# A two-layer hybrid decoder trunk on one core: layers written out, the next layer's input transposed inside the last down projection, weights stored in the order in which they are read, small parameters packed, gate columns moved into the first chunk

## The chip, the core and the metric

The kernel runs on one core of a Trainium2 chip. A core has five engines that run their own instruction streams and meet at semaphores: TensorE (PE, the matrix engine, with a separate row PEld for its weight loads), VectorE (DVE), ScalarE (ACT), GpSimd (POOL) and SyncE (SP). SP only starts DMAs here. The metric is the device time of one execution in microseconds (us); lower is better. The kernel before was timed three times: 2275.53, 2276.73 and 2278.32 us, median 2276.73 us.

## The reference

Input is x (256 tokens by 2048 features, float32), positions, and the parameters of two layers. One layer computes

```
n = rms_norm(x, attn_norm_w)
proj = n @ w_in                      # 2048 -> 6160 columns
   # gla q 512 | k 512 | v 1024 | g 1024 | gate_lr 16 | diff q 1024 | k 1024 | v 1024
y_gla  = gla_mixer(q, k, v, g, gate_lr @ gate_w2 + gate_b)    # chunks of 64 tokens
y_diff = diff_attention(...)         # rotary, softmax 1 - lambda * softmax 2
x = x + concat(y_gla, y_diff) @ w_out        # 2048 -> 2048
n = rms_norm(x, mlp_norm_w)
x = x + relu(n @ w_up)^2 @ w_down            # 2048 -> 8192 -> 2048
```

The 16 gate_lr columns are the low-rank input of the decay gates. All weights are float32 and are read once per execution.

## The kernel before

Each weight matrix is cut into chunks of 512 output columns, and a chunk into pieces of two blocks of 128 rows (KP = 2), 512 KB a piece. A layer has 384 pieces: 96 for w_in (12 chunks), 32 for w_out (8 half-height chunks), and 4 blocks of 64 for the MLP (4 up chunks and 4 down chunks of 8 pieces each).

Float32 accuracy comes from three single-pass products. For every piece SP loads `raw` (4 slots), ACT copies it to a rounded `w_high` (`split`, L656), DVE computes `w_low = raw - w_high` (L920), and PE does 2 row blocks x 2 token tiles x 3 matmuls of 128x512 (L356 to L358): high by high, high by low, low by high. A slot is free for ACT when PE has used the piece that was in it four pieces earlier, and free for SP when DVE has made its low half. The stationary operand is the transposed activation, also as high and low: `xt_high`, `xt_low` for w_in and w_up, `mt_high`, `mt_low` for w_out and w_down. To make it, PE transposes 512 columns of x (8 transposes, L391) into a `side` PSUM buffer, ACT writes the high half times the norm weight (`normed_high`, L682), DVE the low half (`normed_low`, L944). Sums stand in two PSUM accumulators that alternate by chunk; DVE takes them out (`take`, L967; `add_to_x`, L973; L1297).

The order of the work is written out by hand on each engine: `pieces(n)` means "do pieces up to n of this layer", and the attention work stands between such calls.

All engines run a loop over the two layers (`Fori(0, DEPTH)`); inside it the first MLP block is written out and the other three are a loop (`Fori(1, BLOCKS)`). Semaphore waits compare with values computed from the loop registers.

Start of a layer: SP first loads three rows of norm weights (L291), then the first four pieces, then eleven parameter DMAs (L303), among them the 16 gate columns `wlr` (128 KB in runs of 64 bytes) and gate_w2, norm weights and lambda vectors broadcast to 128 partitions; only then come pieces 4 and up. PE transposes the norm rows (L400), then x0 and x1, does pieces 0 and 1, transposes x2, pieces 2 and 3, transposes x3, pieces 4 to 7. DVE waits for all eleven parameter DMAs before it makes `w_low` of piece 2 (L980), ACT before piece 4 (L696). The squares of x for the norm (L706) come after piece 7, since they need the tile `tmp` that holds the lambda vectors.

The gate columns: 48 matmuls with 256 moving columns (L421 to L423) after piece 7, copied by ACT (L713), turned back with a small matmul (`lr_back`, L438), scaled on DVE, and transposed again (L445).

At the boundary of the layers everything above runs again: x1's last columns are ready only when DVE has added the last down chunk to x (L973), and the transposes of the next layer start after that. At the end of the program the last 512 columns of x are added by one DVE operation and stored by one DMA (L329).

Of the kernel before, what the change touches and what calls it, by code (L numbers as in the profile page):

```python
# [52 lines left out]
IN_AT = [c * CW for c in range(LR_COL // CW)] + [LR_COL + RANK + c * CW for c in range(6)]  # L53

CHUNKS = [(IN_CHUNK * c, IN_CHUNK, 0) for c in range(12)]
CHUNKS += [(12 * IN_CHUNK + HALF * k, HALF, (k // 4) * (KT // 2)) for k in range(8)]
MIX_PIECES = 12 * IN_CHUNK + 8 * HALF
BLOCKS = 4
BLOCK_PIECES = 8 * IN_CHUNK
LAYER_PIECES = MIX_PIECES + BLOCKS * BLOCK_PIECES  # L60
BLOCK_CHUNKS = 8
LAYER_CHUNKS = len(CHUNKS) + BLOCKS * BLOCK_CHUNKS

USES = ["nw", "x0", "x1", "x2", "x3", "lr", "gq", "lr_back", "lrT", "z", "gk", "diag"]
USES += [f"level{n}" for n in range(8)]
USES += ["go0", "go1", "dq0", "gy0", "gy1", "dq1", "dk0", "score0", "dk1", "score1", "w0", "score2",
         "do0", "w1", "score3", "do1", "w2", "do2", "w3", "do3", "dy0", "dy1", "m0", "m1", "m2", "m3"]
HUSES = 4 * BLOCKS  # L70
NUSES = len(USES) + HUSES
PAIR = {u: n % 2 for n, u in enumerate(USES)}
NTH = {u: n // 2 + 1 for n, u in enumerate(USES)}
PER_PAIR = [(NUSES + 1 - p) // 2 for p in range(2)]
LEVEL_AT = [27, 30, 33, 37, 41, 45, 49, 52]
NORM_DMAS = 3
PARAM_DMAS = 11
STEPS = {"dve": 160, "act": 40, "pool": 64}


def build(nc, ins, out):
    (x_d, pos_d, anw_d, win_d, w2_d, gb_d, onw_d, qnw_d, knw_d, lq1_d, lk1_d, lq2_d, lk2_d, sub_d,
     wout_d, mnw_d, wup_d, wdn_d, ident_d, maskb_d, lmask_d, scanm_d, invf_d, lamc_d) = ins
# [7 lines left out]
    raw = sb("raw", [P, SLOTS, KP, CW])  # L91
    w_high = sb("w_high", [P, SLOTS, KP, CW], F32R)
    w_low = sb("w_low", [P, SLOTS, KP, CW], F32R)
# [25 lines left out]
    lmask = sb("lmask", [P, 7 * 64 + P])  # L119
# [12 lines left out]
    nw_rows = sb("nw_rows", [36, P])  # L132
    nwt = sb("nwt", [P, 36])
    w2 = sb("w2", [RANK, GH * DK])
    wlr = sb("wlr", [P, KT, RANK])
    onw = sb("onw", [P, DV])
    subw = sb("subw", [P, 256])
    qknw = sb("qknw", [P, 2, P])
    lamc = sb("lamc", [P, 2])
    lam_s = sb("lam_s", [P, 2])  # L140
    lam_e = sb("lam_e", [P, 2])
    nlam = sb("nlam", [P, 1])
# [33 lines left out]
    const_in = sem("const_in")  # L176
# [3 lines left out]
    params_in = sem("params_in")  # L180
    out_in = sem("out_in")
    angle_ready = sem("angle_ready")
# [5 lines left out]
    wlr_h = sem("wlr_h")  # L188
    wlr_ready = sem("wlr_ready")
# [20 lines left out]
    merge_open = sem("merge_open")  # L210
    layer_open = sem("layer_open")
    load_open = sem("load_open")
# [4 lines left out]
    def full(u, layer):  # L217

        return side_full[PAIR[u]], layer * PER_PAIR[PAIR[u]] + NTH[u]

    def done(u, layer):

        return side_done[PAIR[u]], layer * PER_PAIR[PAIR[u]] + (NTH[u] + 1)

    def hpair(c):
        return (len(USES) + c) % 2

    def hnth(c, block, layer):

        p = hpair(c)  # L230
        first = (len(USES) + 1 - p) // 2 + c // 2 + 1
        return layer * PER_PAIR[p] + block * 2 + first

    class Chain:


        def __init__(self, eng, step, per_layer):
            self.eng, self.step, self.per_layer = eng, step, per_layer
            self.layer, self.before, self.n = 0, 0, 0

        def start_layer(self, layer, before):
            self.layer, self.before, self.n = layer, before, 0

        def __call__(self, ins):
            self.n += 1
            assert self.n <= self.per_layer
            ins.then_inc(self.step, 1)
            self.eng.wait_ge(self.step, self.layer * self.per_layer + (self.before + self.n))

        def end_layer(self):  # L250
            if self.per_layer > self.n:
                self.eng.sem_inc(self.step, self.per_layer - self.n)
# [10 lines left out]
    with nc.Block() as block:  # L263
# [3 lines left out]
        def _(sp):  # L267
            sp.dma_start(ident[:], ident_d).then_inc(ident_in, 16)
            win = win_d.rearrange("l (k p) n -> l p k n", p=P)
            wout = wout_d.rearrange("l (k p) n -> l p k n", p=P)  # L270
            wup = wup_d.rearrange("l (k p) n -> l p k n", p=P)
            wdn = wdn_d.rearrange("l (k p) n -> l p k n", p=P)

            def load(n, before, src):

                sp.wait_ge(low_ready, before + (n + 1))
                if n == 0:
                    sp.sem_inc(load_open, 1)
                sp.dma_start(raw[:, n % SLOTS], src).then_inc(raw_in[n % SLOTS], 16)

            with sp.Fori(0, DEPTH) as layer:

                sp.wait_ge(piece_used, layer * (LAYER_PIECES - 6 * SLOTS) + 1)

                def bc(ap):
                    return ap.partition_broadcast(P)
                for dst, src in (
                        (nw_rows[0:16, :], anw_d[layer].rearrange("(k p) -> k p", p=P)),
                        (nw_rows[16:32, :], mnw_d[layer].rearrange("(k p) -> k p", p=P)),
                        (nw_rows[32:36, :], gb_d[layer].rearrange("(k p) -> k p", p=P))):  # L290
                    sp.dma_start(dst, src).then_inc(norms_in, 16)  # L291
                before = layer * LAYER_PIECES
                for n in range(SLOTS):
                    load(n, before, win[layer, :, KP * n:KP * (n + 1), IN_AT[0]:IN_AT[0] + CW])
                for dst, src in (
                        (wlr[:], win[layer, :, :, LR_COL:LR_COL + RANK]),
                        (w2[:], w2_d[layer]),
                        (onw[:], bc(onw_d[layer])), (subw[:], bc(sub_d[layer])),
                        (qknw[:, 0, :], bc(qnw_d[layer])), (qknw[:, 1, :], bc(knw_d[layer])),
                        (lamc[:], bc(lamc_d[layer])),  # L300
                        (tmp[:, 0:128], bc(lq1_d[layer])), (tmp[:, 128:256], bc(lq2_d[layer])),
                        (tmp[:, 256:384], bc(lk1_d[layer])), (tmp[:, 384:512], bc(lk2_d[layer]))):
                    sp.dma_start(dst, src).then_inc(params_in, 16)  # L303
                for c, (first, count, k0) in enumerate(CHUNKS):
                    for i in range(count):
                        k = k0 + KP * i
                        if first + i < SLOTS:
                            continue
                        if c < 12:
                            src = win[layer, :, k:k + KP, IN_AT[c]:IN_AT[c] + CW]  # L310
# [24 lines left out]
        def _(pe):  # L335
            pe.sem_inc(piece_used, SLOTS)

            def piece(n, before, first, count, k0, left, parity, cidx):
# [3 lines left out]
                if i == 0:  # L342

                    pe.wait_ge(acc_done, cidx)
# [1132 lines left out]
```

## Time and profile before

| | |
|---|---|
| median of 3 runs | 2276.73 us |
| span of the profiled execution (first to last instruction) | 2275.6 us |
| lowest of the 3 runs | 2275.53 us |
| PE busy | 2245.0 us (99%), 10342 matmuls |
| DVE busy | 1325.5 us (58%) |
| ACT busy | 1018.9 us (45%) |
| POOL busy | 225.0 us (10%) |
| DMA | 410.67 MB, mean 180 GB/s |

How to read it: the matmuls are pipelined, so the duration of one (390 to 396 ns for 128x512) is longer than the distance between two starts, and the distance is what counts. "Idle before" is the time in which the engine did nothing ahead of the instruction, and the releaser is who ended it. [...] The span and the timed runs agree within 1.1 us.

### The profile page before, as it was taken

Reading aid. Unit: us, or ns where it says so; the run is one execution under the profiler, and the core shown is the slowest. Engines: PE = TensorE matmul, PEld = TensorE weight load, DVE = VectorE, ACT = ScalarE, POOL = GpSimd, SP = SyncE. Lnnn points to the kernel's source line nnn. Section 1 sums busy time; section 2 is a strip of 40 time slices with the busy share of each in tenths; the row PEclk is TensorE's granted clock in tenths of the full one; section 3 lists DMA queues with packets and bytes.
Section 4 is the critical chain, followed back from the end, with each engine's and each line's share of the span. In section 5 each row is a group of like instructions: output and inputs, shape, how many; then the busy total and the mean of one; then the engine's idle time right before and its main releaser. Section 6 shows DMA issues by size and latency. Waiting matters only on the chain.

```text
span 2275.6 us, 29971 instructions
## 1 busy us (share of the span) xinstructions
PE 2245.0 (99%) x10342; PEld 1869.6 (82%) x10342; DVE 1325.5 (58%) x1278; ACT 1018.9 (45%) x1246; POOL 225.0 (10%) x155
## 2 busy tenths in 40 slices
PE   6999999999999999999989999999999999999999
PEld 5888888888888888888878888888888888888887
DVE  4678775655455555555457787756555554555554
ACT  4544454544344344344345445545444443443442
POOL 0034720000000000000001356100000000000000
PEclk9999999999999999999999999999999999999999
DMA  6555655665665665665555656556656666656654
GB/s 206 155 171 153 176 167 171 181 185 190 192 188 189 194 185 186 192 187 189 191 142 166 175 148 178 166 176 185 184 188 193 185 192 192 188 185 193 185 188 161
DMA packets 219099, 410.67 MB, mean 180 GB/s; under 512 B 17672, under 2 KB 20176, under 8 KB 218992
## 3 DMA queue, kind: packets, MB, share of 16 engines
q1 hardware_dynamic: 217056, 406.54, 58.9%
q10 hardware_dynamic: 1936, 2.75, 0.4%
q8 instruction: 60, 0.98, 0.2%
q14 instruction: 47, 0.39, 0.1%
HBM read 407.15 MB, written 2.10 MB: 180 GB/s over the span
## 4 chain that ended last, share of the span: by engine, by line
PE 91%; POOL 4%; issue 3%; SPq 1%; DMA 0%; DVE 0%; ACT 0%; POOLq 0%; DVEq 0%; ACTq 0%
PE acc L356 29%; PE acc L358 29%; PE acc L357 29%; PE side L611 1%; PE side L391 1%; SPq L303 1%; PE side L481 1%; POOL tmp L1418 1%; POOL stage L1423 1%; POOL y L1376 1%; POOL tmp L1419 0%; POOL k_lev L1369 0%; DMA tmp<-in_diff_lambda_k 0%; POOL stage L1411 0%; POOL tmp L1421 0%
## 5 line engine op out<-in xcount | busy, mean ns | idle before, releaser
L920 DVE TENSOR_TENSOR w_low<-raw,w_high 128x1024 fp32r<-128x1024 f32 x768 | 993.9, 1297 | 853.6 <-ACT w_high L656 851.8
L656 ACT ACTIVATE w_high<-raw 128x1024 fp32r<-128x1024 f32 x768 | 812.7, 1060 | 1102.3 <-PE acc L358 1099.6
L356 PE MATMUL acc<-w_high,xt_high 128*128 128x512 f32 x1792 | 709.9, 396 | 16.1 <-DVE w_low L920 16.1
L358 PE MATMUL acc<-w_high,xt_low 128*128 128x512 f32 x1792 | 701.3, 391 | 0.0
L357 PE MATMUL acc<-w_low,xt_high 128*128 128x512 f32 x1792 | 700.6, 391 | 0.0
L356 PE MATMUL acc<-w_high,mt_high 128*128 128x512 f32 x1280 | 502.1, 392 | 0.0
L358 PE MATMUL acc<-w_high,mt_low 128*128 128x512 f32 x1280 | 498.9, 390 | 0.0
L357 PE MATMUL acc<-w_low,mt_high 128*128 128x512 f32 x1280 | 498.4, 389 | 0.0
L356 PEld LDWEIGHTS acc<-w_high,xt_high 128*128 128x128 f32 x1792 | 338.5, 189 | 85.6 <-DVE w_low L920 17.0
L358 PEld LDWEIGHTS acc<-w_high,xt_low 128*128 128x128 f32 x1792 | 338.0, 189 | 71.3
L357 PEld LDWEIGHTS acc<-w_low,xt_high 128*128 128x128 f32 x1792 | 338.7, 189 | 68.2
L358 PEld LDWEIGHTS acc<-w_high,mt_low 128*128 128x128 f32 x1280 | 240.3, 188 | 50.2
L357 PEld LDWEIGHTS acc<-w_low,mt_high 128*128 128x128 f32 x1280 | 240.5, 188 | 49.2
L356 PEld LDWEIGHTS acc<-w_high,mt_high 128*128 128x128 f32 x1280 | 240.4, 188 | 49.0
L1335 POOL TENSOR_TENSOR xrs<-xss,eps 128x2 f32<-128x2 f32 x4 | 0.8, 196 | 932.8 <-ACT tmp L706 772.4
L973 DVE TENSOR_TENSOR x<-acc,x 128x1024 f32<-128x1024 f32 x48 | 58.7, 1223 | 30.0 <-PE acc L358 30.0
L1297 DVE TENSOR_SCALAR stage<-acc,xrs 128x512 f32<-128x512 f32 x64 | 45.1, 747 | 12.9 <-PE acc L358 12.9
L944 DVE SCALAR_TENSOR_TENSOR xt_low<-side,nwt,xt_high 128x256 fp32r<-128x256 f32 x64 | 26.5, 477 | 31.0 <-ACT xt_high L682 26.8
L896 ACT ACTIVATE stage<-stage 128x1024 f32<-128x1024 f32 x32 | 34.0, 1062 | 12.3 <-DVE stage L1297 12.3
L1306 DVE TENSOR_TENSOR mt_low<-side,mt_high 128x1024 fp32r<-128x1024 f32 x32 | 39.0, 1218 | 0.0
L682 ACT ACTIVATE xt_high<-side,nwt 128x256 fp32r<-128x256 f32 x64 | 24.9, 474 | 26.8 <-PE side L391 26.8
L611 PEld LDWEIGHTS side<-ident,stage 128*128 128x128 f32 x256 | 29.8, 140 | 4.2
(160 smaller groups left out, 909.5 us busy)
## 6 DMA issues: line engine op xcount, KB each, us to landing
raw<-in_w_up SPq DMA_DIRECT2D x256, 512.0 KB, 3.7
raw<-in_w_down SPq DMA_DIRECT2D x256, 512.0 KB, 3.6
raw<-in_w_in SPq DMA_DIRECT2D x192, 512.0 KB, 3.8
raw<-in_w_out SPq DMA_DIRECT2D x64, 512.0 KB, 3.7
x<-in_x ACTq DMA_DIRECT2D x4, 512.0 KB, 7.4
out<-x SPq DMA_DIRECT2D x4, 512.0 KB, 5.1
lmask<-c_lmask ACTq DMA_DIRECT2D x1, 288.0 KB, 10.6
wlr<-in_w_in SPq DMA_DIRECT2D x2, 128.0 KB, 8.9
```

Of the source, the lines that this page charges most:

```text
L356: pe.matmul(o, a_high, w_high[:, s, kk, :], start=start, stop=False)
L357: pe.matmul(o, a_high, w_low[:, s, kk, :], start=False, stop=False)
L358: last = pe.matmul(o, a_low, w_high[:, s, kk, :], start=False, stop=stop)
L611: last = pe.transpose(side[p][:, j * SEQ + t * P:j * SEQ + (t + 1) * P], stage[:, c % 2, t, j * P:(j + 1) * P], ident[:])
L656: act.activation(w_high[:, n % SLOTS], raw[:, n % SLOTS], ACT.Copy).then_inc(high_ready, 1)
L682: last = act.activation(xt_high[:, 4 * c + j, :], s[:, j * SEQ:(j + 1) * SEQ], ACT.Copy, scale=nwt[:, w0 + 4 * c + j:w0 + 4 * c + j + 1])
L896: act.activation(stage[:, c % 2], stage[:, c % 2], ACT.Square).then_inc(relu_h, 1)
L920: dve.tensor_tensor(w_low[:, n % SLOTS], raw[:, n % SLOTS], w_high[:, n % SLOTS].bitcast(F32), ALU.subtract).then_inc(low_ready, 1)
L944: last = dve.scalar_tensor_tensor(out=xt_low[:, k, :], in0=s[:, j * SEQ:(j + 1) * SEQ], scalar=nwt[:, w0 + k:w0 + k + 1], in1=xt_high[:, k ...
L973: dve.tensor_tensor(cols, acc[parity][:], cols, ALU.add).then_inc(acc_done, 1)
L1297: last = dve.tensor_scalar(stage[:, c % 2, t, :], acc[c % 2][:, t, :], xrs[:, 1, t:t + 1], 0.0, ALU.mult, ALU.max)
L1306: dve.tensor_tensor(mt_low[:, 4 * c:4 * c + 4, :].rearrange("p a b -> p (a b)"), side[hpair(c)][:], mt_high[:, 4 * c:4 * c + 4, :].rearran ...
```

## The change

It does five things.

1. The loops over layers and MLP blocks are gone: every engine's stream is written out, and every semaphore wait compares with a constant.
2. In the last MLP block of layer 0, PE transposes columns 0 to 1535 of the next layer's x (x0, x1, x2) in the middle of the last three down chunks, with ACT's and DVE's halves of it behind. Only x3 is left for after the last down chunk, and PE does piece 0 of the next layer before it. The squares of x come after piece 3, not after piece 7.
3. The host stores each weight matrix so that a piece is one contiguous run per partition (4 KB). The memory distance between two partitions of one piece becomes the whole length of a layer's row: 385 KB for w_in, 128 KB for w_out, 512 KB for w_up and w_down. Before, a piece was 256 runs of 2 KB, with rows 24, 8, 32 and 8 KB apart.
4. Norm weights come transposed and packed (one DMA, no PE transpose); the four broadcast parameters come as one `wide` tile, the lambda vectors as one 512 KB tile already repeated for 128 partitions. All but the norms are issued by POOL, most of them after PE has used three pieces. The DMAs of layer 1's parameters are issued during layer 1 after its first norm.
5. The 16 gate columns stand in front of w_in's columns. The first 528 columns (16 gate, 512 q) become two chunks of 264 columns, each in 4 pieces of 4 row blocks. Piece numbers from 8 on mean the same columns as before. `lr` and `lr_back` are gone; DVE takes the gate columns from the accumulator, and PE transposes them once (lrT).

At the end the last add and the last store are split by token tile. The core of the diff:

```diff
-IN_AT = [c * CW for c in range(LR_COL // CW)] + [LR_COL + RANK + c * CW for c in range(6)]
+Q_HALF = (CW - RANK) // 2
+SLOT = 4 * (RANK + Q_HALF)
+IN_AT = [0, RANK + Q_HALF] + [RANK + CW * (c + 1) for c in range(11)]
+IN_N = [RANK + Q_HALF, CW - Q_HALF] + [CW] * 11
+    chunks = [("in", IN_AT[c], IN_N[c], 0, KT, 4 if c < 2 else KP) for c in range(13)]
...
@@ sync
-            with sp.Fori(0, DEPTH) as layer:
-                sp.wait_ge(piece_used, layer * (LAYER_PIECES - 6 * SLOTS) + 1)
...
+            sp.dma_start(norms[:].rearrange("p l k -> p (l k)"), norms_d).then_inc(norms_in, 16)
+            def load(n):
+                layer, (c, k, kp) = n // LAYER_PIECES, PIECES[n % LAYER_PIECES]
+                name, at, cols, k0, _, _ = CHUNKS[c]
+                rows = KT * BLOCKS if name == "down" else KT
+                first = at * rows + (k0 + k) * cols
+                if n >= SLOTS:
+                    sp.wait_ge(low_ready, n - SLOTS + 1)
+                sp.dma_start(raw[:, n % SLOTS, 0:kp * cols],
+                             weights[name][layer, :, first:first + kp * cols]).then_inc(raw_in[n % SLOTS], 16)
+            load(0)
+            sp.dma_start(ident[:], ident_d).then_inc(ident_in, 16)
+            for n in range(1, DEPTH * LAYER_PIECES):
+                load(n)
@@ tensor
-                s = open_side("lr")
-                pe.wait_ge(wlr_ready, layer + 1)
-                for k in range(KT):
-                    pe.matmul(s[:, 0:SEQ], mt_high[:, k, 0:P], xt_high[:, k, :], start=k == 0, stop=False)
...
+                if layer == 0:
+                    pe.wait_ge(ident_in, 16)
+                    for c in range(3):
+                        pe.wait_ge(x_in[c], 16)
+                        transpose_chunk(f"x{c}", x[:, :, c * CW:(c + 1) * CW])
+                        if c:
+                            pieces(c, {c - 1: f"x{c - 1}"})
+                    pe.wait_ge(x_in[3], 16)
+                else:
+                    pieces(1, {0: "x0"})
+                    pe.wait_ge(*taken(layer - 1, LAYER_CHUNKS - 1))
                 transpose_chunk("x3", x[:, :, 3 * CW:4 * CW])
+                pieces(4, {n: f"x{n}" for n in range(4)})
+                pieces(8)
                 chunk_taken(0)
                 s = open_side("lrT")
...
+                            if i == 3 and c >= 5 and blk == BLOCKS - 1 and layer + 1 < DEPTH:
+                                chunk_taken(LAYER_CHUNKS - 9 + c)
+                                transpose_chunk(f"x{c - 5}", x[:, :, (c - 5) * CW:(c - 4) * CW], layer + 1)
@@ scalar
+                if layer == 0:
+                    act.wait_ge(norms_in, 16)
+                    for c in range(4):
+                        normed_high(f"x{c}", c, 0, 0)
+                        pieces(c + 1)
+                else:
+                    pieces(3)
+                    normed_high("x3", 3, 0, layer)
+                    pieces(4)
+                    act.wait_ge(*taken(layer - 1, LAYER_CHUNKS - 1))
                 for t in range(T):
                     act.activation(squared(t), x[:, t, :], ACT.Square, ...).then_inc(x_ss, 1)
+                    pieces(5 + t)
@@ vector
+                else:
+                    pieces(3)
+                    add_to_x(layer - 1, LAYER_CHUNKS - 1, 3)
+                    pieces(4)
+                    normed_low("x3", 3, 0, layer)
+                pieces(7)
                 dve.wait_ge(x_rs, layer * 2 + 1)
+                dve.wait_ge(*summed(layer, 0))
+                for t in range(T):
+                    dve.tensor_scalar(lr_s[:, t, :], acc[parity(layer, 0)][:, t, 0:RANK], ...)
+                    last = dve.tensor_scalar(stage[:, 0, t, 0:Q_HALF], ...)
+            for t in range(T):
+                xs = x[:, t, 3 * CW:]
+                dve.tensor_tensor(xs, acc[...][:, t, :], xs, ALU.add).then_inc(last_half, 1)
@@ gpsimd
+            pool.dma_start(lamc[:].rearrange("p l m -> p (l m)"), lamc_d).then_inc(lamc_in, 16)
+            pool.dma_start(att[:, 0:1024], lam_d).then_inc(lam_in, 16)
+            pool.wait_ge(piece_used, SLOTS + 3)
+            pool.dma_start(w2[:], w2_d[0]).then_inc(w2_in, 16)
...
+            pool.dma_start(maskb[:], maskb_d).then_inc(maskb_in, 16)
```

## Rows read from the trace of the kernel before

**Rows 1.** Busy time by stretch: stretch, length, then busy (count) per engine, clock, DMA, GB/s.
```profile
13.00:56.60 43.60, 33.79 (x161) 28.59 (x162) 23.17 (x35) 20.62 (x30) 1.79 (x3) 0.92 0.62 184
56.60:1143.40 1086.80, 1086.30 (x4996) 904.00 (x4994) 638.33 (x603) 487.17 (x588) 108.80 (x70) 1.00 0.60 181
1143.40:1184.20 40.80, 34.61 (x179) 29.54 (x179) 24.45 (x36) 22.01 (x35) 1.79 (x3) 0.87 0.55 155
```
**Rows 2.** Waits of the whole span: who waited for whom, total us, times, longest.
```profile
ACT w_high L656 <- PE acc L358: 1099.6, 698, 3.5
PE acc L356 <- DVE w_low L920: 16.1, 3, 7.1
PE side L400 <- DMA nw_rows<-in_gla_gate_b: 8.9, 1, 8.9
ACT w_high L656 <- DMA raw<-in_w_in: 2.4, 4, 1.1
```
**Rows 3.** Timeline, PE alone, 43 to 57 us: start, length, engine, line.
```profile
43.33 0.39 PE L356 MATMUL acc<-w_high,xt_high 128*128 128x512 f32 x1
...
50.13 0.39 PE L356 MATMUL acc<-w_high,xt_high 128*128 128x512 f32 x1
...
50.81 0.28 PE L421 MATMUL side<-xt_high,mt_high 128*128 128x256 f32 x1
50.81 0.19 PEld L422 LDWEIGHTS side<-xt_low,mt_high 128*128 128x128 f32 x1
...
56.20 0.28 PE L421 MATMUL side<-xt_high,mt_high 128*128 128x256 f32 x1
```
**Rows 4.** Timeline of the first 35 us.
```profile
6.82 11.19 SPq L303 DMA_DIRECT2D w<-in_gla_gate_w  x1
9.21 3.65 PE L391 MATMUL side<-ident,x 128*128 128x128 f32 x16
12.85 1.66 DVE L944 SCALAR_TENSOR_TENSOR xt_low<-side,nwt,xt_high 128x256 fp32r<-128x256 f32 x4 [12.85 <-ACT xt_high L682]
14.42 2.35 DVE L920 TENSOR_TENSOR w_low<-raw,w_high 128x1024 fp32r<-128x1024 f32 x2
14.43 1.06 ACT L656 ACTIVATE w_high<-raw 128x1024 fp32r<-128x1024 f32 x1 [0.67 <-DMA raw<-in_w_in]
15.39 1.55 ACT L682 ACTIVATE xt_high<-side,nwt 128x256 fp32r<-128x256 f32 x4
15.69 0.80 PE L356 MATMUL acc<-w_high,xt_high 128*128 128x512 f32 x1 [2.84 <-DVE w_low L920]
...
17.14 0.63 PE L356 MATMUL acc<-w_high,xt_high 128*128 128x512 f32 x1
...
18.42 0.63 PE L356 MATMUL acc<-w_high,xt_high 128*128 128x512 f32 x1
...
23.90 1.03 PE L391 MATMUL side<-ident,x 128*128 128x128 f32 x8
...
29.99 0.43 DVE L980 TENSOR_TENSOR tmp<-tmp 128x256 f32<-128x256 f32 x1 [11.36 <-DMA tmp<-in_diff_lambda_k]
...
32.05 0.79 PE L356 MATMUL acc<-w_high,xt_high 128*128 128x512 f32 x1 [7.12 <-DVE w_low L920]
```
**Rows 5.** DMA issues: x in the first 1.3 us, w_up over the span.
```profile
x<-in_x ACTq DMA_DIRECT2D x2, 512.0 KB, 5.9
...
raw<-in_w_up SPq DMA_DIRECT2D x256, 512.0 KB, 3.7
```
**Rows 6.** Timeline around the layer boundary.
```profile
1148.99 1.66 DVE L944 SCALAR_TENSOR_TENSOR xt_low<-side,nwt,xt_high 128x256 fp32r<-128x256 f32 x4 [4.23 <-issue]
...
1151.84 0.80 PE L356 MATMUL acc<-w_high,xt_high 128*128 128x512 f32 x1 [6.16 <-DVE w_low L920]
```
**Rows 7.** Timeline: the gate's way back (PE), and the program's end (DVE).
```profile
63.00 0.61 PE L438 MATMUL side<-ident,lr_t 16*128 16x16 f32 x4
...
2271.14 1.22 DVE L973 TENSOR_TENSOR x<-acc,x 128x1024 f32<-128x1024 f32 x1 [8.56 <-PE acc L358]
```

More of the change, by code:

```diff
@@ L425, in _ @@
-                last.then_inc(full_sem("lr"), 1)
-                pieces(10)
-                def chunk_taken(c):
-                    pe.wait_ge(acc_done, layer * LAYER_CHUNKS + (2 + c + 1))
-                chunk_taken(0)
-                transpose_chunk("gq", stage[:, 0])
-                s = open_side("lr_back")
-                pe.wait_ge(*done("lr", layer))
-                for t in range(T):
-                    last = pe.matmul(s[:, t * CW:t * CW + RANK], lr_t[:, t * P:(t + 1) * P],
-                                     ident[0:RANK, 0:RANK], start=True, stop=True)
@@ L440, in _, with chunk_taken @@
[L440 to L441 removed]
+                    last.then_inc(full_sem(u, of), 1)
+                def chunk_taken(c):
+                    pe.wait_ge(*taken(layer, c))
+                if layer == 0:
+                    pe.wait_ge(ident_in, 16)
+                    for c in range(3):
+                        pe.wait_ge(x_in[c], 16)
[6 more added lines that the diff above has]
+                    pe.wait_ge(*taken(layer - 1, LAYER_CHUNKS - 1))
@@ L925, in _ @@
+            for layer in range(DEPTH):
                 at = [0]
@@ new lines, in _ @@
+                last.then_inc(acc_done, 1)
+                pieces(9)
+                if layer == 0:
+                    dve.wait_ge(lamc_in, 16)
+                    dve.wait_ge(lam_exp, 1)
+                    for of in range(DEPTH):
+                        dve.scalar_tensor_tensor(out=nlam[:, of:of + 1], in0=lam_e[:, of, 1:2],
+                                                 scalar=lamc[:, of, 0:1], in1=lam_e[:, of, 0:1],
+                                                 op0=ALU.subtract, op1=ALU.subtract)
@@ L1016, in _ @@
-                c3 = float(np.float32(two_pi - c1 - c2))
-                for c in (c1, c2, c3):
-                    link(dve.scalar_tensor_tensor(out=ang, in0=turns, scalar=-c, in1=ang,
-                                                  op0=ALU.mult, op1=ALU.add))
-                pieces(14)
-                s = source("lr_back")
-                for t in range(T):
-                    last = dve.tensor_scalar(lr_s[:, t, :], s[:, t * CW:t * CW + RANK],
-                                             xrs[:, 0, t:t + 1], None, ALU.mult)
```

814 lines of the change are left out of this document (375 added, 439 removed).

## The prediction, made before the changed kernel was run

> **What bounds the kernel now.** I read the busy time by stretch first, cut at the places that the change touches. From 56.6 to 1143.4 us PE is busy 1086.30 of 1086.80 us at clock 1.00; the second layer's same stretch has the same length. The two stretches in which a layer starts are different: 13.0 to 56.6 us has 33.79 of 43.60 us busy at clock 0.92, 1143.4 to 1184.2 us has 34.61 of 40.80 at 0.87 [rows 1]. So the rest of the program is the count of matmuls times their distance, and only these two places, the end, and the number and width of the matmuls can move the time. The waits say the same: ACT waits 1099.6 us for PE to free a slot and 2.4 us for weight DMAs, and PE's own waits on `w_low` are 16.1 us in 3 times, all at layer starts [rows 2]. DVE and ACT cost nothing where they have cover.
>
> The price of a matmul is its distance to the next. Thirty 128x512 matmuls lie between the starts 43.33 and 50.13: 226.7 ns each. Forty-five of 256 columns lie between 50.81 and 56.20: 119.8 ns each [rows 3]. The difference, 106.9 ns for 256 columns, is 0.4176 ns a column, so 264 columns come to 119.8 + 8 x 0.4176 = 123.1 ns. A PE transpose chunk of eight inside a stream costs about 0.80 us: seven distances of 0.109 us and the two changes of kind, from the eight that take 1.03 us with the last one's drain [rows 4].
>
> **Start, part by part.** Before, the work of the first accumulator chunk and the gate ends at 56.56, just after the last row of [rows 3]. In it are 96 x 0.2267 + 48 x 0.1198 = 27.5 us of matmuls and 1.6 us of transposes; the rest is waiting and the half clock (the starts 17.14 and 18.42 are three matmuls apart, 427 ns each) [rows 4]. What held it: PE waited for the norm rows until 8.9 us [rows 2], 2.84 us for the first `w_low`, and 7.12 us at 32.05, since DVE stood until 29.99 for the lambda DMAs; those came late because SP stood 11.19 us on issue 6.82, behind the 64-byte gate columns [rows 4]. Written so, the next waits are these. x0 landed some 5.9 us after an issue at 0.7 to 1.3 [rows 5], so x0's transposes can start near 6.5 instead of 9.21, with `ident` and the norms as one DMA in by then. From there I step with the durations of [rows 4]: eight cold transposes 1.8 (half of 3.65), ACT's high half 1.6, DVE's low half 1.7, DVE's `w_low` 1.2 to 1.3 (half of 2.35, for 1056 elements 3% more): piece 0 at about 13.0 instead of 15.69. Piece 0 is 24 x 0.22 = 5.3 us at the half clock. x2's transposes stand behind it, then piece 1 (24 x 0.1231 = 2.95 us), x3's, and pieces 2 and 3 each wait for the chain ACT 1.6, DVE 1.7, DVE 1.3 behind the transposes: they start near 24.4 and 28.2, with 1 us lost ahead of each. Pieces 4 to 7 need 11.8 us more, the two squares on ACT and the products of lambda on DVE lie in the 2.95 us of a piece. Chunk 1 ends at 28.2 + 2.95 + 11.8 = 43.0. That is 13.6 us less; 3.9 us of it is plain PE work: 192 x 0.1231 = 23.6 against 27.5.
>
> What could be late next here: POOL issues seven DMAs between piece 2 and its rsqrt for `xrs`, and DVE waits for `xrs` before it takes chunk 0, with `w_low` of piece 7 queued behind, and PE behind that. In the trace POOL issues none. The nearest issues are those of SP and ACT, 0.3 to 0.9 us, with one of 11.19 [rows 4]. Seven at the short end end before x's squares do and cost 0. If each took 2 us, `xrs` would be some 5 us late for piece 7. I take 0, nearest to the ordinary issue, and keep 0 to 5. Landing order adds: the lambda tile is 512 KB instead of 256, beside x and the first pieces, but `lmask`, `maskb` and `scanm` leave this window; I keep -1 to +4 for it.
>
> **Layer boundary.** Before: 40.8 us from the last down matmul to the end of the gate [rows 1], with 6.16 us of waiting: DVE makes the low half at 1148.99 after 4.23 us in which nothing that the profile shows held it, and PE restarts at 1151.84 on the half clock [rows 6]. After: PE goes from the last down matmul into piece 0, whose x0 was made three chunks earlier; DVE adds x's last columns (1.22 us, [rows 7]) in piece 0's 2.95 us. x3's transposes end at 3.75, piece 1 at 6.7, piece 2 at 9.65; x3's halves are ready after ACT 1.6, ACT `w_high` 1.1, DVE `w_low` 1.3 and DVE 1.7, in that order on the two engines: about 9.6. That is a tie; I take 0.3 us of stall and keep 0 to 1.5. So the stretch is 192 x 0.1231 + 0.80 + 0.3 = 24.7 us, 16.1 us less; the other three transpose chunks move into the last down chunks, where each has whole pieces of cover on ACT and DVE, and cost PE 3 x 0.80 = 2.4. Net -13.7 us. No idle time means no half clock. In layer 1 DVE waits for `wide` after piece 8; POOL issues it after the rsqrt at about 13 us past the boundary, DVE comes there at 18, and PE would feel it at 24.5: covered, and with 3 us over it even if the landing is doubled.
>
> [...]
>
> **Smaller parts.** `lr_back`: four tiny matmuls and two changes of kind, 0.70 us a layer (start 63.00, the next weight matmul 0.55 us later, and a dearer step before it) [rows 7]: -1.4 us. The written-out MLP blocks, constant waits and the packed norms after the start: 0, covered by a busy PE; a gain is excluded by the 0.5 us that PE is idle in 1086.8 [rows 1], a loss only if instructions come late. Last add and store by halves: the 1.22 us add [rows 7] releases its first half after 0.65, the second store is half as large; -0.5, between 0 and -1. Contiguous weight runs: 0, because landing takes 3.7 us [rows 5] and ACT waits for PE and not for data [rows 2]; below nothing is excluded by the same waits, above see the rival.
>
> **Sum,** against the profiled execution (span 2275.6 us, which the timed runs exceed by -0.1 to 2.7, the median by 1.1): -13.6 -13.7 -1.4 -0.5 = -29.2, so a span of 2246.4. With the median's 1.1 us, and 0.5 us for the half of the POOL and landing bounds that I don't dismiss, I predict **2248 us**.
>
> **Rivals.**
> (a) *The start gives back part.* POOL's issues or the landing of x and pieces 0 to 3 decide: +4 to +10, so 2252 to 2258; for it: everything in the first 15 us shares one set of DMA engines, and POOL's issue price is unknown. Against: less data is wanted early than before.
> (b) *The boundary doesn't do what it says.* If the fetch of code, not the loop end, held DVE for 4.23 us, or x3's chain is longer, PE waits once more and drops to the half clock: up to 6 us of stall and 3 us of slow matmuls come back, 2257.
> (c) *Narrow matmuls are held by weight loads.* A load is shown with 0.19 us [rows 3]. At 190 ns instead of 123 the 384 narrow ones cost 384 x 0.067 = 26 us more, and the time is 2274. Against: the 256-column ones run at 119.8 ns beside the same 0.19 us loads, so loads overlap.
> (d) *Slower: the new memory distances.* [...] A piece lasts PE 12 x 0.2267 = 2.72 us, so 193 GB/s are needed; the kernel runs at 181 with 0.60 of the DMA engines' time [rows 1], so there is room up to about 300. It decides only if the rate falls by more than a third. At 183 GB/s, 5% short, each of the 512 MLP pieces takes 0.14 us longer: +73, a time of 2321. Against: nothing in the trace; for it: it can't be seen there, since the old rows were 8 to 32 KB apart.
>
> [...]
>
> **Chances.** The forecast 0.75 (own range 2242 to 2254), (a) 0.10, (b) 0.04, (c) 0.03, (d) 0.06, and 0.02 for another loss such as late instructions. The range 2241 to 2259 leaves (c), (d) and the edges out, and takes in POOL's 5, landing's -1 to 4 and the boundary's 1.5. No change means within 0.2%, 4.6 us, about what a measurement of this kernel can tell. Faster by more: the first three cases, 0.89. Within: (c), 0.03, and a little of the rest, 0.04. Slower: (d) and late instructions, 0.07.
>
> **What would show it.** The stretch to the first 512-column matmul after the gate columns ends near 43 us instead of 56.6, with POOL's last DMA issue ahead of its first rsqrt; narrow matmuls start 0.123 us apart; x3's chunk stands 3 us after the last down matmul and PE's clock stays at 1.00 there; PE waits for `w_low` under 3 us in all; weight pieces land in about 3.7 us for w_up and w_down too, and ACT still waits for PE. A landing of over 8 us in the MLP, or ACT waiting for DMAs there, would prove (d) and the forecast wrong; a long middle stretch (over 1089 us) with PE idle would too.

## The result and the profile after

The changed kernel takes 2281.31 us (median of 18 runs, 2280.33 to 2282.22) against 2277.85 us for the kernel before (18 runs, 2275.53 to 2279.65). The ratio is 1.0016, 95% interval 1.001 to 1.0023: slower by 0.16%, within the 0.2% that the prediction called no change. I had forecast 2248 us. The profiled execution has a span of 2279.2 us.

Here is the busy time by stretch of the changed kernel, cut at the same places in the work as [rows 1]: start to the end of the narrow chunks, the rest of layer 0, the second layer's narrow chunks, the rest of layer 1. The columns are those of [rows 1].

```profile
13.00:46.90 33.90, 28.09 (x211) 27.69 (x211) 22.51 (x36) 20.62 (x32) 6.55 (x10) 0.90 0.61 211
46.90:1150.00 1103.10, 1103.10 (x5015) 905.89 (x5013) 646.91 (x619) 494.07 (x602) 108.42 (x70) 1.00 0.54 180
1150.00:1174.50 24.50, 24.50 (x203) 24.43 (x202) 13.82 (x18) 13.41 (x16) 2.99 (x5) 1.00 0.56 191
1174.50:2275.00 1100.50, 1100.50 (x4991) 903.19 (x4988) 633.49 (x588) 484.78 (x584) 108.92 (x70) 1.00 0.54 178
```

The two places that were to be mended are mended: the start ends at 46.9 instead of 56.6 us, the layer boundary takes 24.5 us instead of 40.8, with PE busy throughout at clock 1.00 (before, the clock stood at 0.50 from 1149 to 1156 us). The loss is in the two long stretches, where only +1.7 and -0.7 us were to happen: 1103.1 and 1100.5 us instead of 1086.8 each [rows 1]. PE isn't idle there at all, and weight loads are busy for 903 to 906 us as before (904). So it isn't a wait that was added: the same matmuls take longer. The waits of the changed kernel (who waited for whom, total us, times, longest) leave no other place. PE itself waits little; what has grown is ACT's wait for PE, from 1099.6 us [rows 2]:

```profile
ACT w_high L593 <- PE acc L334: 1136.9, 702, 3.5
PE side L362 <- DMA ident<-c_ident: 9.3, 1, 9.3
PE acc L332 <- DVE w_low L849: 6.3, 3, 4.7
ACT w_high L593 <- DMA raw<-in_w_in: 3.0, 2, 1.7
```

The distance between two starts shows it. This is PE's timeline of the changed kernel from 603 us: one piece in slot 3, then the start of the next, in slot 0 (start, length, engine, line).

```profile
603.28 0.40 PE L332 MATMUL acc<-w_high,mt_high 128*128 128x512 f32 x1
603.52 0.39 PE L333 MATMUL acc<-w_low,mt_high 128*128 128x512 f32 x1
...
604.67 0.40 PE L332 MATMUL acc<-w_high,mt_high 128*128 128x512 f32 x1
604.91 0.39 PE L333 MATMUL acc<-w_low,mt_high 128*128 128x512 f32 x1
605.14 0.40 PE L334 MATMUL acc<-w_high,mt_low 128*128 128x512 f32 x1
605.38 0.39 PE L332 MATMUL acc<-w_high,mt_high 128*128 128x512 f32 x1
...
606.07 0.39 PE L332 MATMUL acc<-w_high,xt_high 128*128 128x512 f32 x1
606.31 0.40 PE L333 MATMUL acc<-w_low,xt_high 128*128 128x512 f32 x1
...
607.00 0.39 PE L333 MATMUL acc<-w_low,xt_high 128*128 128x512 f32 x1
607.22 0.39 PE L334 MATMUL acc<-w_high,xt_low 128*128 128x512 f32 x1
607.45 0.39 PE L332 MATMUL acc<-w_high,xt_high 128*128 128x512 f32 x1
607.68 0.39 PE L333 MATMUL acc<-w_low,xt_high 128*128 128x512 f32 x1
```

The piece in slot 3 takes 606.07 - 603.28 = 2.79 us for 12 matmuls, with distances that alternate between 0.24 and 0.22 or 0.23; from its fourth matmul on the next piece goes on at 0.227. Averaged from the start times of this trace over 600 to 1000 us, the distance is 227.9, 232.7, 228.1 and 232.6 ns in slots 0 to 3, and 226.7 to 227.2 in all four before. These means leave out the nine steps of some 313 ns in that stretch at which PE comes back from other work. The change made a slot 1056 elements long (4 row blocks of 264 columns), 4224 bytes, where it was 4096. So slots 1 and 3 start 128 bytes off a multiple of 256, counted from the start of the tile. I saw no other property that tells odd from even slots; whether it is the cause is for the experiments.

### The profile page after: what moved, and what is told of

The parts are those of the page before. It is cut to its first block, busy times and chain, and to the rows that moved or that the text cites. A ratio compares the mean times of both kernels' runs of the same rounds, so it can differ in the third digit from the quotient of the medians.

```text
span 2279.2 us, 25481 instructions
## 1 busy us (share of the span) xinstructions
PE 2259.6 (99%) x10428; PEld 1864.2 (82%) x10428; DVE 1318.0 (58%) x1263; ACT 1014.5 (45%) x1235; POOL 228.5 (10%) x164
## 4 chain that ended last, share of the span: by engine, by line
PE 99%; DMA 0%; DVE 0%; ACT 0%; issue 0%; SPq 0%; DVEq 0%; ACTq 0%
PE acc L332 31%; PE acc L334 31%; PE acc L333 31%; PE side L362 1%; PE side L552 1%; PE side L427 1%; DMA ident<-c_ident 0%; PE side L479 0%; PE side L398 0%; PE side L412 0%; PE side L478 0%; PE side L496 0%; PE side L447 0%; PE side L498 0%; PE side L445 0%; PE side L439 0%
## 5 line engine op out<-in xcount | busy, mean ns | idle before, releaser
L849 DVE TENSOR_TENSOR w_low<-raw,w_high 128x1024 fp32r<-128x1024 f32 (+1 forms) x768 | 993.1, 1295 | 889.1 <-ACT w_high L593 888.2
L593 ACT ACTIVATE w_high<-raw 128x1024 fp32r<-128x1024 f32 (+1 forms) x768 | 813.3, 1061 | 1139.9 <-PE acc L334 1136.9
L332 PE MATMUL acc<-w_high,xt_high 128*128 128x512 f32 (+1 forms) x1856 | 723.4, 390 | 6.3 <-DVE w_low L849 6.3
L334 PE MATMUL acc<-w_high,xt_low 128*128 128x512 f32 (+1 forms) x1856 | 716.3, 386 | 0.0
L333 PE MATMUL acc<-w_low,xt_high 128*128 128x512 f32 (+1 forms) x1856 | 714.9, 385 | 0.0
L332 PEld LDWEIGHTS acc<-w_high,xt_high 128*128 128x128 f32 x1856 | 349.9, 188 | 77.7 <-issue 7.5
L334 PEld LDWEIGHTS acc<-w_high,xt_low 128*128 128x128 f32 x1856 | 349.3, 188 | 73.8
L333 PEld LDWEIGHTS acc<-w_low,xt_high 128*128 128x128 f32 x1856 | 349.9, 189 | 71.6
L899 DVE TENSOR_TENSOR x<-acc,x 128x1024 f32<-128x1024 f32 x47 | 57.5, 1223 | 13.6 <-PE acc L334 13.6
L862 DVE SCALAR_TENSOR_TENSOR xt_low<-side,norms,xt_high 128x256 fp32r<-128x256 f32 x64 | 26.5, 478 | 24.0 <-ACT xt_high L605 24.0
L552 PE MATMUL side<-ident,stage 128*128 128x128 f32 x256 | 33.1, 272 | 0.0
```

Source lines behind the costliest of these rows:

```text
L332: pe.matmul(o, a_high, w_high[:, n % SLOTS, w], start=start, stop=False)
L333: pe.matmul(o, a_high, w_low[:, n % SLOTS, w], start=False, stop=False)
L334: last = pe.matmul(o, a_low, w_high[:, n % SLOTS, w], start=False, stop=stop)
L552: last = pe.transpose(s[:, j * SEQ + t * P:j * SEQ + (t + 1) * P], stage[:, c % 2, t, j * P:(j + 1) * P], ident[:])
L593: act.activation(w_high[:, n % SLOTS, 0:size], raw[:, n % SLOTS, 0:size], ACT.Copy).then_inc(high_ready, 1)
L849: dve.tensor_tensor(w_low[:, n % SLOTS, 0:size], raw[:, n % SLOTS, 0:size], w_high[:, n % SLOTS, 0:size].bitcast(F32), ALU.subtract).then_ ...
```

## The experiments

Each was compared with the kernel before on the same chip. Addresses stand in no view: where I give a tile's start, it is an estimate from the tile sizes, with each tile directly behind the one before it in the kernel's text and `raw` on a multiple of 256. Where I give the mean distance, it is that between main matmuls, averaged as above from the trace's start times over 600 to 1000 us. Over all slots it is 226.8 ns in the kernel before and 230.3 in the changed kernel; their difference is the 3.5 ns from which the expectations up to e4 are worked out. The same can be read without arithmetic from the count of matmuls that PE starts in this stretch, in brackets behind its busy time. These are the kernel before, the changed kernel and e1_w1088:

```profile
600.00:1000.00 400.00, 400.00 (x1802) 332.06 (x1801) 208.78 (x180) 170.73 (x163) 0.00 (x0) 1.00 0.62 189
600.00:1000.00 400.00, 400.00 (x1776) 326.97 (x1775) 206.11 (x179) 168.46 (x160) 0.00 (x0) 1.00 0.56 187
600.00:1000.00 400.00, 400.00 (x1803) 331.89 (x1802) 209.04 (x181) 170.64 (x163) 0.00 (x0) 1.00 0.57 189
```

**e1_w1088, only the slot pitch mended.**

```diff
-    w_high = sb("w_high", [P, SLOTS, SLOT], F32R)
-    w_low = sb("w_low", [P, SLOTS, SLOT], F32R)
+    w_high = sb("w_high", [P, SLOTS, 1088], F32R)
+    w_low = sb("w_low", [P, SLOTS, 1088], F32R)
```

> The changed kernel with one number changed: the slots of w_high and w_low lie 1088 elements (4352 bytes) apart instead of 1056 (4224), so that every slot starts on a multiple of 256 bytes; raw keeps 1056. In the changed kernel's trace the 512-column matmuls are 232.6 ns apart in slots 1 and 3 (start 128 bytes off a multiple of 256) and 227.9 in slots 0 and 2. Theory A, the start address of the moving operand costs it: all slots near 226.8 ns, 9024 matmuls x 3.5 ns = 32 us less, about 2250 us. Theory B, the new memory layout of the weights (runs of 4 KB) or the fetch of the written-out code slows TensorE: no change, 2281. Theory C, the pitch of raw, which DMA writes and ACT and DVE read, disturbs TensorE: no change, 2281.

Measured: 2251.98 us, ratio to before 0.9892 (0.9875 to 0.9908). Mean distance 226.8 ns (226.7 to 227.2 by slot); the odd slots, 256 bytes off a multiple of 512, aren't slower. The long stretches are back, and the rest is as in the changed kernel (busy time by stretch of this run):

```profile
13.00:46.80 33.80, 27.93 (x209) 27.53 (x210) 22.51 (x36) 20.69 (x32) 6.55 (x10) 0.90 0.61 203
46.80:1135.30 1088.50, 1088.14 (x5015) 905.81 (x5013) 648.32 (x619) 494.02 (x602) 108.92 (x70) 1.00 0.57 182
1135.30:1159.60 24.30, 24.30 (x203) 24.23 (x202) 13.81 (x18) 13.40 (x16) 2.99 (x5) 1.00 0.59 195
1159.60:2245.40 1085.80, 1085.42 (x4991) 903.13 (x4988) 634.99 (x588) 484.70 (x584) 108.92 (x70) 1.00 0.56 181
```

Raw kept its pitch, and the memory layout and the written-out code stayed: rivals B and C fall for the changed kernel.

This run also shows where no cost appears. In the narrow chunks a row block is 1056 bytes long, so blocks 1 to 3 of a piece start 32, 64 and 96 bytes off. In this run's narrow chunks at the layer boundary, matmuls of blocks 0 to 3 stand 122.0, 121.0, 120.6 and 121.7 ns from the next (averaged from the start times): the offset blocks aren't slower. In the changed kernel, with 128 bytes more in the odd slots, the mean of these matmuls is 122.2 ns against 121.3 here. So what follows is measured for 512 columns.

**e2_before_w1056, the same fault put into the kernel before.** The tiles become one flat row with a pitch.

```diff
-    w_high = sb("w_high", [P, SLOTS, KP, CW], F32R)
-    w_low = sb("w_low", [P, SLOTS, KP, CW], F32R)
+    w_high = sb("w_high", [P, 3 * 1056 + 1024], F32R)
+    w_low = sb("w_low", [P, 3 * 1056 + 1024], F32R)
...
```

> The kernel before with its w_high and w_low slots 1056 elements apart instead of 1024, and nothing else. Theory A: slots 1 and 3 go to 232 to 234 ns, slots 0 and 2 stay at 226.8 to 228, 9216 x 3.5 ns = 32 us more, about 2309 us. Theory B (memory layout, code): no change, 2277. Theory C (raw): no change.

Measured: 2309.35 us, ratio 1.0145 (1.0128 to 1.0162). The size is right, the picture isn't: slots 0 to 3 are at 230.6, 228.7, 232.6 and 230.8 ns, so the even slots, which theory A wants fast, are slow too. The mean over all slots is 230.7 ns, and 1769 matmuls start from 600 to 1000 us, against 1802 before. The tile sizes tell what else moved, by the estimate above: w_high's tile is now 16768 bytes, 128 off a multiple of 256, so w_low behind it starts 128 bytes off, and its even slots are the offset ones; behind both tiles x, xt and mt are back on multiples of 256. In every slot one of the two w tiles is off. That the time hit theory A's number is therefore no proof of A: half of the pairs are off in either picture.

**e3_before_raw1056, only raw's pitch.**

```diff
-    raw = sb("raw", [P, SLOTS, KP, CW])
+    raw = sb("raw", [P, 3 * 1056 + 1024])
...
```

> The kernel before with only raw's slots 1056 elements apart. Theory A: no change, 2277 within 2 us. Theory C: about 30 us more, with slots 1 and 3 slow.

Measured: 2276.82 us, ratio 0.9998 (0.9988 to 1.0008), distance 226.8 ns, with slots 1 and 3 at 226.7. C falls here as well. But this run says more than I had planned. Raw's tile is 16768 bytes, 128 off a multiple of 256, so by the same estimate w_high, w_low, xt and mt all start 128 bytes off. All moving operands are off, and nothing is slow. Theory A as I put it is refuted.

**e4_before_low1056, only w_low's pitch.**

```diff
-    w_low = sb("w_low", [P, SLOTS, KP, CW], F32R)
+    w_low = sb("w_low", [P, 3 * 1056 + 1024], F32R)
...
```

> The kernel before with only w_low's slots 1056 elements apart, so one matmul in three has a moving operand 128 bytes off in slots 1 and 3. Theory A: a third of the 32 us, about +10 us (2287), and in the trace the distance after the w_low matmuls of odd slots is longer. If instead one badly placed operand disturbs its neighbours as much, up to +30.

Measured: 2314.0 us, ratio 1.0163 (1.0146 to 1.018); slots 0 to 3 at 231.8, 231.0, 231.8 and 230.6 ns, 231.3 over all, with 1765 matmuls from 600 to 1000 us. A third of the moving operands got the new pitch, and the loss is larger than with all of them, outside both numbers that I had given. The estimate from the sizes offers a reason: w_low's tile pushes xt and mt 128 bytes off, and now all pairs with w_high and those with w_low's even slots disagree, five in six.

**e5_stat128, the stationary operands moved instead.** From here on the theory (A2) is that the distance modulo 256 between the two operands counts.

```diff
+    pad = sb("pad", [P, 32])
...
```

It stands between w_low and x, and nothing reads it.

> The kernel before with an unused tile of 128 bytes per partition between w_low and x, so that x, xt and mt move by 128 bytes and the weight slots stay on multiples of 256 bytes. The run with only raw's pitch changed had moved w_high, w_low, xt and mt together by 128 bytes off a multiple of 256 and was not slower, so theory A as I put it (the moving operand's own start) doesn't hold alone. Theory A2, it is the distance modulo 256 bytes between the moving operand (w) and the stationary one (xt, mt): all slots slow, between 231 ns (even slots of the run with w_low's pitch changed) and 233.4 ns (odd slots of the changed kernel), +4.5 to +6.6 ns x 9216 = +41 to +61 us, about 2318 to 2338. Theory A, the moving operand's own start counts: no change, 2277.

Measured: 2324.25 us, ratio 1.0208 (1.0191 to 1.0225), all four slots at 232.2 to 232.6 ns. An unused tile of 128 bytes costs 47 us. A2 holds, A doesn't. The same stretch from 600 to 1000 us, this run first, e3_before_raw1056 second; busy PE and clock say nothing, the count and the weight loads' busy time do:

```profile
600.00:1000.00 400.00, 400.00 (x1757) 325.23 (x1756) 202.75 (x175) 165.29 (x158) 0.00 (x0) 1.00 0.60 185
```

```profile
600.00:1000.00 400.00, 400.00 (x1802) 331.97 (x1802) 208.77 (x180) 170.64 (x162) 0.00 (x0) 1.00 0.61 189
```

**e6_w1040 and e7_w1032, how far off is off.** Both w tiles get a pitch of 4160 or 4128 bytes and a length of 4160 elements (16640 bytes), so that what follows stays on multiples of 256.

```diff
+    w_high = sb("w_high", [P, 4160], F32R)
+    w_low = sb("w_low", [P, 4160], F32R)
+    RAW, HIGH, LOW = 1024, 1040, 1040
...
```

In e7_w1032 the last two numbers are 1032.

> The kernel before with w_high and w_low slots 1040 elements (4160 bytes) apart, each tile padded so that w_low and xt start on multiples of 256 bytes: slots 0 to 3 are 0, 64, 128 and 192 bytes off xt modulo 256. A2 with a grain of 64 bytes or less: slot 0 at 226.7 ns, slot 2 as the odd slots of the changed kernel (232 to 233), slots 1 and 3 slow as well by some amount. A2 with a grain of 128 bytes only: slots 1 and 3 like a neighbour. Time 2290 to 2320 us.

> As the run before, with 1032 elements (4128 bytes): slots 0 to 3 are 0, 32, 64 and 96 bytes off. If any offset that isn't 0 modulo 256 costs, slots 1, 2 and 3 are all near 232 ns and the time is 2277 + 9216 x 0.75 x 5 ns = 2312. If only 128 costs, all are at 226.8 and the time is 2277.

Measured, one run each: 2313.85 and 2319.01 us. Distances by the slot's offset to xt:

```
offset modulo 256 bytes   0      32     64     96     128    192
ns between starts, e6     228.7         230.3         232.7  233.0
ns between starts, e7     229.8  233.6  229.9  234.2
```

Slot 0 is slow only in its earlier matmuls, as in the timeline above, behind a slow slot; its last ones are at 226.7. So a slot's mean holds something of the slot before it, and the figures are no exact price of one offset. Every offset tried costs 3 to 7.5 ns a matmul, and 32 and 96 cost most. e7 missed its 2312 us by 7, upwards: slots 1 and 3 cost more than the 5 ns that I had put, and slot 0 wasn't free. e6 is inside its range.

**e8_no_early_turn, the moved transposes undone in the aligned kernel.**

```diff
-                            if i == 3 and c >= 5 and blk == BLOCKS - 1 and layer + 1 < DEPTH:
...
-                                chunk_taken(LAYER_CHUNKS - 9 + c)
-                                transpose_chunk(f"x{c - 5}", x[:, :, (c - 5) * CW:(c - 4) * CW], layer + 1)
...
-                    pieces(1, {0: "x0"})
                     pe.wait_ge(*taken(layer - 1, LAYER_CHUNKS - 1))
+                for c in range(3):
+                    pe.wait_ge(x_in[c], 16)
+                    transpose_chunk(f"x{c}", x[:, :, c * CW:(c + 1) * CW])
...
```

ACT and DVE change with it.

> The aligned kernel (slots 1088 apart) with the second layer started as the first: x0 to x3 are transposed after the last down chunk, and the squares stay after piece 3. It undoes only the moved transposes. Theory: they are worth 10 to 14 us (restart some 7 us after the last down matmul, half clock for a few us, 1 us of wait ahead of pieces 2 and 3, against 2.4 us more of transposes in the down chunks), so 2262 to 2266 against 2252. Rival: they are worth nothing, since the chain through DVE and ACT is as long either way: 2252.

Measured: 2261.43 us, ratio 0.9929 (0.9912 to 0.9946): the moved transposes are worth 9.5 us beside e1 (two chips; the spans differ by 9.7), a little under the range. By stretches of the two traces it is 12.6 us less at the boundary and 2.7 us more in the down chunks. PE's timeline at the boundary (with what ended the idle time) shows the wait that comes back, and the granted clock falls: it is 0.50 from 1140.0 to 1144.8 us, where the matmuls of 264 columns stand 0.22 apart:

```profile
1134.03 1.97 PE L362 MATMUL side<-ident,x 128*128 128x128 f32 x16 [1.39 <-DVE x L886]
1139.87 0.56 PE L332 MATMUL acc<-w_high,xt_high 128*128 128x264 f32 x1 [3.87 <-DVE w_low L836]
```

The boundary stretch is 37.1 us here, against 41.1 in the kernel before, so 4.0 of its 16.5 us come from the rest of the change. The gate columns in the first chunks account for it alone: 192 narrow matmuls instead of 96 of 512 columns and 48 of 256 were to save 3.9 us of PE work. Written-out code and fewer, earlier parameters show no gain of their own at the boundary.

**e9_aligned_again.** The kernel of e1 once more, beside the next two.

> The aligned kernel again (the changed kernel with w_high and w_low slots 1088 elements apart), beside the next two on the same chip: 2252 us within 1.

Measured: 2251.09 us, ratio 0.9887 (0.9871 to 0.9904).

**e10_start, the start in order.**

```diff
+            sp.dma_start(ident[:], ident_d).then_inc(ident_in, 16)
             sp.dma_start(norms[:].rearrange("p l k -> p (l k)"), norms_d).then_inc(norms_in, 16)
...
             load(0)
-            sp.dma_start(ident[:], ident_d).then_inc(ident_in, 16)
...
+            act.wait_ge(const_ready, 1)
+            act.activation(junk[:, 0, 0:8], eps[:], ACT.Copy)
...
+            pool.wait_ge(piece_used, SLOTS + 1)
             pool.dma_start(att[:, 0:1024], lam_d).then_inc(lam_in, 16)
```

> The aligned kernel with three things moved at the start: ident is the first DMA (in the changed kernel it landed at 9.2 us behind the first weight piece, while x0 was in at 5.4), the 512 KB of lambda vectors are issued after PE has used piece 0, and one small activation ahead of the first wait loads ACT's table (1.28 us that stood between x0's transposes and their high half). Theory, the start is a chain and not a rate: x0's transposes at 5.6 instead of 9.3, piece 0 at 12 to 13 instead of 17.3, 3 to 5 us less than the aligned kernel: 2247 to 2249. Rival, the start is bound by the landing of x and the first pieces at 400 GB/s: no more than 1 us, 2251.

Measured: 2246.01 us (2245.34 to 2246.72), ratio 0.9864 (0.9848 to 0.9881): 5.1 us less than e9 on the same chip, and the fastest version, 31 us ahead of the kernel before. The forecast of 3 to 5 us is met at its upper end, and the rival's 1 us isn't. The rate that the rival names is in the traces (406, 398, 381 and 413 GB/s in the steps of 2 us from 6 to 14 us of the changed kernel; 384, 411 and 420 from 8 to 14 here), and the start got shorter all the same. The three edits were made together, so their shares aren't separated. The changed kernel's first matmuls and this run's:

```profile
9.27 3.28 PE L362 MATMUL side<-ident,x 128*128 128x128 f32 x16 [9.27 <-DMA ident<-c_ident]
17.29 0.56 PE L332 MATMUL acc<-w_high,xt_high 128*128 128x264 f32 x1 [4.75 <-DVE w_low L849]
```

```profile
2.79 1.28 ACT L584 ACT_TABLE_LOAD   x1 [2.79 <-issue]
4.97 1.94 PE L362 MATMUL side<-ident,x 128*128 128x128 f32 x8 [4.97 <-DMA x<-in_x]
11.80 0.56 PE L332 MATMUL acc<-w_high,xt_high 128*128 128x264 f32 x1 [2.44 <-DVE w_low L851]
```

**e11_old_layout, the memory layout undone in the aligned kernel.**

```diff
-                rows = KT * BLOCKS if name == "down" else KT
-                first = at * rows + (k0 + k) * cols
...
-                sp.dma_start(raw[:, n % SLOTS, 0:kp * cols],
-                             weights[name][layer, :, first:first + kp * cols]).then_inc(raw_in[n % SLOTS], 16)
+                src = weights[name].rearrange("l (k p) n -> l p k n", p=P)
+                sp.dma_start(raw[:, n % SLOTS, 0:kp * cols].rearrange("p (k n) -> p k n", k=kp),
+                             src[layer, :, k0 + k:k0 + k + kp, at:at + cols]).then_inc(raw_in[n % SLOTS], 16)
...
```

> The aligned kernel with the weight matrices in memory as before (only the gate columns moved to the front of w_in), so that a piece is again 256 runs of 2 KB, or 512 of 1 KB for the narrow chunks. It undoes the layout part alone. Theory, the transfers have cover either way: landing goes from 3.4 back to 3.7 us and the time stays at 2252 within 2. Rival, the new layout is worth something through the start or through TensorE's reads beside DMA writes: over 3 us slower, 2255 or more.

Measured: 2253.07 us, ratio 0.9897 (0.9881 to 0.9914), 2.0 us over e9, as forecast. The ratios' intervals overlap, but both hold the spread of the kernel before; the four runs of each version on this chip don't (2252.42 to 2253.67 against 2250.83 to 2251.14), so the new layout seems to be worth 1 to 2 us. In the single traces it lies at the start: piece 0 starts 1.6 us later (18.98 against 17.38), the first 512-column matmul 1.3 us later, and the stretches behind are equal. The w_up pieces land as in [rows 5]:

```profile
raw<-in_w_up SPq DMA_DIRECT2D x256, 512.0 KB, 3.7
```

**e12_low_stationary, who disturbs whom.**

```diff
+    pad0 = sb("pad0", [P, 32])
     xt_low = sb("xt_low", [P, KT, SEQ], F32R)
+    pad1 = sb("pad1", [P, 32])
```

> The kernel before with 128 unused bytes ahead of xt_low and 128 behind it: xt_low alone is 128 bytes off, xt_high, mt and all weight slots are on multiples of 256 bytes. In the w_in and up chunks every third matmul (L360 here, high weights by xt_low) has an offset stationary operand; the w_out and down chunks have none and are the control at 226.7 ns. If the weight load of a matmul is disturbed by, and disturbs, the matmul that streams meanwhile, the distance from the w_low matmul before it (L359) to it grows, by 5 to 20 ns; if it is the matmul with the offset operand itself, the distance from L360 to the next L358 grows. Time 2277 + 5376/3 x 5 to 20 ns: 2286 to 2313 us.

Measured, one run: 2296.97 us. The timeline of PE in an up chunk, where every third stationary operand (xt_low, L360) is off:

```profile
700.26 0.40 PE L359 MATMUL acc<-w_low,xt_high 128*128 128x512 f32 x1
700.49 0.40 PE L360 MATMUL acc<-w_high,xt_low 128*128 128x512 f32 x1
700.72 0.39 PE L358 MATMUL acc<-w_high,xt_high 128*128 128x512 f32 x1
700.95 0.40 PE L359 MATMUL acc<-w_low,xt_high 128*128 128x512 f32 x1
701.18 0.40 PE L360 MATMUL acc<-w_high,xt_low 128*128 128x512 f32 x1
```

From 600 to 1000 us the means are: L359 to L360 232.4 ns, L360 to L358 234.0, L358 to L359 227.1; with mt in the down chunks of the same run 226.6, 226.9 and 226.5. So both distances beside the offset operand grow, and the test doesn't choose between the weight load that runs beside the stream of the matmul before and the one that runs beside its own. It does show, in one run, that only the matmuls next to the offset operand pay.

## Why the prediction was wrong

Set against e1_w1088, which differs from the changed kernel by nothing but the pitch, the steps of the prediction come out so (starts of the main matmuls in the traces):

| step | predicted | measured |
|---|---|---|
| start, to the first piece after the narrow chunks | 56.6 to 43.0, -13.6 | to 46.8, -9.7 |
| rest of layer 0: lr_back out, three transpose chunks in | +1.7 | 1086.55 to 1088.26, +1.7 |
| layer boundary | 24.7 us, -16.1 | 41.07 to 24.53 (24.70 in the changed kernel), -16.5 |
| rest of layer 1: lr_back | -0.7 | 1086.53 to 1085.52, -1.0 |
| the end | -0.5 | 4.89 to 4.42, -0.5 |
| distance of the 512-column matmuls | unchanged, 0 | changed kernel against e1: +14.6 and +14.7 |

**The step that failed** is the premise in the first paragraph of the prediction, that outside the mended places "the rest of the program is the count of matmuls times their distance", with the distance taken from [rows 3] and kept. The count was right and the distance wasn't: between 600 and 1000 us 226.8 became 230.3 ns, and over the two long stretches the loss is 29.3 us, 3.2 ns in each of 9024 matmuls, while e1's other steps add up to -26.0. Together +3.3, and the spans differ by 3.6; the rest is 0.2 at the boundary and 0.1 at the start. None of the rivals had it either, and the sign named for a wrong forecast, a middle stretch of over 1089 us, came with PE busy and not idle. I had listed what each edit adds, moves and takes away in time, but not what it does to addresses: `SLOT = 4 * (RANK + Q_HALF)` stood in the diff, and I read it as room for wider pieces.

**The start** was the second miss: its gain was over-estimated by 3.9 us. With the pitch mended the kernel takes 2252 us where 2248 was forecast. The term that was off is "`ident` and the norms as one DMA in by then": x0 landed in time, at 5.4, but ident was issued behind the first weight piece and landed at 9.2, and ACT's table load of 1.28 us, which the sum has nowhere, now stood behind that wait. PE waited for `w_low` 6.3 us in all, 4.7 of it ahead of piece 0; I had named under 3 as the sign of being right. e10 puts both right and starts piece 0 at 11.8, where I had 13.0. The half clock that the prediction puts at the start before is read from distances alone, 427 ns a matmul [rows 4] against 226.7 [rows 3]: the clock column gives 1.00 from 15 to 20 us of that trace. In the changed kernel it gives 0.50 from 16 to 22 us, with matmuls of 264 columns 0.22 us apart.

**What held.** The narrow matmuls' 123.1 ns: they stand 122.2 apart at the changed kernel's boundary and 121.3 at e1's, so rival (c) didn't come. The +1.7 for the rest of layer 0 was met by luck: `lr_back` was worth 1.0 and not 0.7, as layer 1 shows, so the three transpose chunks cost about 2.7 and not 2.4, and the two errors cancel. POOL's seven DMAs took 0.52 to 0.57 us each, and its rsqrt at 35.5 us was in time, so rival (a)'s POOL part didn't come; its other half, late landing, is the start's miss, though what landed late was ident and not x0 or piece 0. Rival (b) didn't come. What held DVE for 4.23 us before [rows 6] no run shows; in e8, with x0's transposes behind the last add again, DVE stands 2.92 us there, and ACT's high half ends it. Rival (d) didn't either: with 512 KB between partitions the up and down pieces land in 3.4 us instead of 3.7, the changed kernel has ACT waiting 3.0 us for data in all, and e11 without the new layout isn't faster. So at a mean of 180 GB/s no run shows a cost of partitions 512 KB apart. Code written out cost nothing that shows: e1 carries all of it, with the long stretches as short as the sum has them.

**The mechanism, and what stays open.** Shown, with the addresses estimated from the tile sizes: the cost follows the difference of the start addresses of moving and stationary operand modulo 256 bytes (e3 moves both, 226.8 ns and no cost; e5 moves one, 232.4 ns and 47 us; 256 bytes in e1, 226.8 ns and no cost), and it is paid by the matmuls beside the offset operand (e12: 232.4 and 234.0 ns, against 227.1 for the third distance). Not shown: what in the chip makes the two operands' addresses matter to each other, whether offsets under 32 bytes matter, why the distances alternate as they do, and what sets the size. The pair alone doesn't set it: in e2 slots 0 and 2 have the same offsets and stand at 230.6 and 232.6 ns. ACT's and DVE's work on the weight slots is no rival: e5 and e12 leave raw and both w tiles where they were.

## What to carry to other kernels

When a tile's size changes, write down the start address modulo 256 bytes of every operand that TensorE reads, for every buffer of a rotation and for every tile behind it; here the change saved 26.0 us of waits and work and lost 29.3 us with its slots 128 bytes off. In a kernel with PE busy at 99%, compare the distance between two matmul starts, or the count in a fixed stretch, since PE's busy time and clock look the same with 1757 matmuls in 400 us as with 1802. At a kernel's start follow one chain (identity, first input tile, table load, first piece) and order the DMAs by it.

## What the runs showed of the hardware that I had not expected

Matmuls of 128x512 in float32r (the kernel's rounded high and low halves) with a new stationary operand each stand 226.8 ns apart on average if moving and stationary operand agree modulo 256 bytes by the tile sizes (the kernel before, e1, e3), and 230 to 234 ns apart if they don't (offsets of 32, 64, 96, 128 and 192 bytes; e5, e6, e7). PE's busy time, its waits and the granted clock hide it; the weight loads' busy time in a fixed stretch (325 to 327 us against 332) and ACT's wait for PE (1136.9 us against 1099.6) do move. Narrow matmuls of 264 columns at offsets of 32, 64 and 96 bytes stood 120.6 to 121.7 ns apart, no slower than the aligned ones at 122.0. An unused tile of 128 bytes made the kernel before 2.1% slower.
